# One expert's weights buffered ahead of the ring, copied in by VectorE, with the block work on ScalarE and GpSimd

## The reference

```python
e_idx = g_idx[:, None] * EXPERTS_PER_GROUP + loc        # top-1 group, top-2 experts in it, of 16
w = jnp.take_along_axis(scores, e_idx, axis=1); w = w / w.sum(-1, keepdims=True)
for e in range(N_EXPERTS):
    g_, u_ = jnp.split(t @ w_gu[e], 2, axis=-1)          # w_gu[e]: 1024 x 1024
    out = out + gates[:, e:e+1] * ((silu(g_) * u_) @ w_dn[e])   # w_dn[e]: 512 x 1024
```

## Time and profile before

| | |
|---|---|
| Median of 3 runs | 2003.49 us (1999.81 to 2008.18) |
| The profiled execution | 2015.61 us, its span 2013.8 us |
| Busy: PE, DVE, ACT, POOL | 1714.7, 641.6, 331.9, 129.3 us |
| Blocks of layer 0 | from about 809 to 1193 us of the span |
| Blocks of layer 1 | from about 1680 to 1981 us |

### The profile page before, as it was taken

The page is one execution under the profiler, slowest core; times in us unless marked ns, Lnnn a source line. Parts: engine busy times, 40 slices in busy tenths (PEclk is TensorE's granted clock), DMA queues, the critical chain, the costliest instruction groups (busy, mean ns, idle before and its releaser), DMA issues.

```text
span 2013.8 us, 29796 instructions
## 1 busy us (share of the span) xinstructions
PE 1714.7 (85%) x12508; PEld 1001.9 (50%) x12508; DVE 641.6 (32%) x1538; ACT 331.9 (16%) x730; POOL 129.3 (6%) x149
## 2 busy tenths in 40 slices
PE   5999999999999996789877755999989976777852
PEld 2454566554444585344433324767778863333311
DVE  3089336671110136101100005764641133000003
ACT  1001135521000102111110101014520020110100
POOL 0200000000000001111111110000000001111100
PEclk9999999999999997999989976999999987899976
DMA  9524545602123324674489984332015534889894
GB/s 308 139 84 140 195 157 184 192 23 87 54 72 94 104 76 184 247 299 159 158 312 350 365 281 133 108 104 74 1 52 160 171 133 163 342 326 361 340 365 152
DMA packets 188823, 365.06 MB, mean 181 GB/s; under 512 B 23285, under 2 KB 107773, under 8 KB 187923
## 3 DMA queue, kind: packets, MB, share of 16 engines
q1 hardware_dynamic: 176784, 331.48, 46.9%
q0 software_dynamic: 10704, 25.16, 3.6%
q10 hardware_dynamic: 1203, 6.51, 0.9%
HBM read 356.79 MB, written 14.42 MB: 184 GB/s over the span
## 4 chain that ended last, share of the span: by engine, by line
PE 67%; DMA 20%; DVE 7%; SPq 3%; ACT 2%; issue 1%; another core or an unknown queue 0%; DVEq 0%; POOLq 0%; ACTq 0%
PE psum L782 64%; DMA ring<-in_moe_w_gu 14%; DMA ring<-in_moe_w_dn 3%; SPq L669 2%; SPq L645 1%; PE psum L966 1%; PE psum L1176 1%; DMA arena<-ys 1%; DMA ring<-in_w_mod 1%; DVE arena L1802 1%; PE psum L1199 0%; PE psum L844 0%; ACT uT L1290 0%; DVE H L2058 0%; DMA ys<-qkT,y_row 0%
## 5 line engine op out<-in xcount | busy, mean ns | idle before, releaser
L782 PE MATMUL psum<-uT,ring 128*128 128x512 f32 (+1 forms) x1472 | 505.2, 503 | 3.3 <-ACT uT L1290 3.3
L782 PE MATMUL psum<-ring,mo_tok 128*32 128x256 f32 x4992 | 351.9, 408 | 110.3 <-DMA ring<-in_moe_w_gu 104.4
L782 PEld LDWEIGHTS psum<-uT,ring 128*128 128x128 f32 x1472 | 281.1, 192 | 222.8 <-issue 204.1
L782 PEld LDWEIGHTS psum<-ring,mo_tok 128*32 128x32 f32 x4992 | 145.7, 114 | 267.3 <-DMA ring<-in_moe_w_gu 167.7
L782 PE MATMUL psum<-ring,v_tok 128*32 128x256 f32 x2496 | 177.2, 419 | 33.3 <-DMA ring<-in_moe_w_dn 26.9
L2032 DVE TENSOR_TENSOR qkT<-psum,qkT 128x128 f32<-128x128 f32 x78 | 22.8, 292 | 404.8 <-ACT qkT L1493 280.1
L782 PEld LDWEIGHTS psum<-ring,v_tok 128*32 128x32 f32 x2496 | 81.3, 121 | 119.2 <-DMA ring<-in_moe_w_dn 46.9
L1672 DVE SCALAR_TENSOR_TENSOR convT<-upad,cwT,convT 128x512 f32<-128x512 f32 (+1 forms) x240 | 132.4, 614 | 2.1
L736 POOL DMA_INDIRECT ys<-qkT,y_row x78 | 77.4, 992 | 592.3 <-ACT qkT L1500 572.0
L782 PE MATMUL psum<-ring,uT 128*128 128x256 f32 (+1 forms) x576 | 113.7, 357 | 0.0
L1500 ACT ACTIVATE qkT<-psum,mqk 128x256 f32<-128x256 f32 x78 | 37.0, 474 | 457.6 <-PE psum L782 457.6
(11 more groups left out here) (284 smaller groups left out, 1428.2 us busy)
## 6 DMA issues: line engine op xcount, KB each, us to landing
ring<-in_moe_w_gu SPq DMA_DIRECT2D x256, 512.0 KB, 7.5
ring<-in_moe_w_dn SPq DMA_DIRECT2D x128, 512.0 KB, 6.7
ring<-in_w_in SPq DMA_DIRECT2D x104, 512.0 KB, 4.7
ring<-in_w_mod SPq DMA_DIRECT2D x96, 512.0 KB, 6.2
ring<-in_w_out SPq DMA_DIRECT2D x16, 512.0 KB, 4.5
ring<-in_w_a_out SPq DMA_DIRECT2D x8, 512.0 KB, 3.5
ring<-in_w_b_out SPq DMA_DIRECT2D x8, 512.0 KB, 4.5
ring<-in_w_c_out SPq DMA_DIRECT2D x16, 256.0 KB, 3.0
```

The costliest lines, as they stand in the source:

```text
L782: return nc.tensor.matmul(dst, lhsT, rhs, start=start, stop=stop)
```

## The change

- Twelve staging buffers of a part each are laid over `yab`, `uT` and `arena`. SyncE fills them for expert 1 as soon as the last reader of each is done (the last branch projection, the last transposes of the tokens, the stored token rows), and for expert e > 1 once part x of expert e-1 has been copied out. Expert 0 goes straight into the ring as before.
- VectorE copies each part from staging into the ring once it is staged (`w_staged[x]`) and the last block of the expert before has used that part (`w_used[x]`), and counts up `w_loaded[x]`. It reads `blocks_to` for that, once an expert, where SyncE did.
- ScalarE also copies the up half of the block from PSUM to SBUF (`gated_blk`), does `hidden_copy`, and both halves of each quad copy but the first, whose second half stays on VectorE.
- GpSimd does the product `hidden`, out of SBUF, one block ahead of the store in its queue.
- `r_cover`, a scratch row of the routing, moves from `yab` to `convT`.

```diff
+        gated_blk = qkT[:, 2, 2 * P:4 * P].rearrange("p (u c) -> p u c", u=2)
+        staging = [buf[:, 2 * x:2 * x + 2, :].rearrange("p a b -> p (a b)") for buf in (yab, uT, arena) for x in range(4)]
...
-        r_cover = yab[0:1, 0:2, :].rearrange("p a b -> p (a b)")[:, 0:MAX_BLOCKS * NE].rearrange("p (b e) -> p b e", e=NE)
+        r_cover = convT[0:1, 0:2, :].rearrange("p a b -> p (a b)")[:, 0:MAX_BLOCKS * NE].rearrange("p (b e) -> p b e", e=NE)
...
-                for e in range(NE):
-                    if e == 1:
-                        sp.wait_ge(counted, l + 1)
-                    if e:
-                        before_e = sp.value_load(blocks_to[0:1, e - 1:e], min_val=1, max_val=n_blocks[l])
+                for x in range(NX):
+                    n = index[("expert", l, x // 2)]
+                    if x % 2 == 0:
+                        sp.wait_ge(stream[n - NS][1], stream[n - NS][2])
+                    sp.dma_start(ring[:, n % NS, (x % 2) * D:(x % 2 + 1) * D], parts[x][0]).then_inc(w_loaded[x], 16)
+                nt = token_tiles(l)
+                for e in range(1, NE):
                     for x in range(NX):
-                        n = index[("expert", l, x // 2)]
-                        if e:
-                            sp.wait_ge(w_used[x], before_e + blk_base[l])
-                        elif x % 2 == 0:
-                            sp.wait_ge(stream[n - NS][1], stream[n - NS][2])
-                        sp.dma_start(ring[:, n % NS, (x % 2) * D:(x % 2 + 1) * D], parts[x][e])\
-                            .then_inc(w_loaded[x], 16)
+                        if e > 1:
+                            sp.wait_ge(w_loaded[x], 16 * (NE * l + e))
+                        elif x == 0:
+                            wait_ready(sp, "yb", l, KD - 1)
+                        elif x == 4:
+                            wait_ready(sp, "nat", l, nt - 1, 1)
+                        elif x == 8:
+                            for t in range(nt):
+                                sp.wait_ge(us_stored[t], 16 * (l + 1))
+                        sp.dma_start(staging[x], parts[x][e]).then_inc(w_staged[x], 16)
...
+                def hidden(b):
+                    u = b % 2
+                    pool.wait_ge(silu_ready, base + b + 1)
+                    if b >= 2:
+                        pool.wait_ge(hidT_ready, base + b - 1)
+                    nc.gpsimd.tensor_tensor(hid_blk[:, u, :], gated_blk[:, u, :], silu_blk[:, u, :], ALU.mult)\
+                        .then_inc(up_drained, 1)
+
+                hidden(0)
                 for b in range(nb):
+                    if b + 1 < nb:
+                        hidden(b + 1)
...
-                    f(silu_blk[:, b % 2, :], psum[G_BANK[b % 2]][:, 0:P], ACT.Silu).then_inc(silu_ready, 1)
+                    f(silu_blk[:, b % 2, :], psum[G_BANK[b % 2]][:, 0:P], ACT.Silu)
+                    f(gated_blk[:, b % 2, :], psum[G_BANK[b % 2]][:, P:2 * P], ACT.Copy).then_inc(silu_ready, 1)
...
+                        hidden_copy(b - 1)
                     if b % QUAD == 0 and b // QUAD + 1 < nquad:
-                        quad_copy(b // QUAD + 1)
+                        quad_copy(b // QUAD + 1, 0)
+                        quad_copy(b // QUAD + 1, 1)
...
+                dve.wait_ge(counted, l + 1)
+                for e in range(1, NE):
+                    before_e = dve.value_load(blocks_to[0:1, e - 1:e], min_val=1, max_val=n_blocks[l])
+                    for x in range(NX):
+                        dve.wait_ge(w_staged[x], 16 * ((NE - 1) * l + e))
+                        dve.wait_ge(w_used[x], before_e + blk_base[l])
+                        n = index[("expert", l, x // 2)]
+                        v.tensor_copy(ring[:, n % NS, (x % 2) * D:(x % 2 + 1) * D], staging[x]).then_inc(w_loaded[x], 16)
```

More of the change, by code:

```diff
@@ L449, in build @@
         w_loaded = [sem(f"expert_part_loaded{x}") for x in range(NX)]
+        w_staged = [sem(f"expert_part_staged{x}") for x in range(NX)]
         w_used = [sem(f"expert_part_used{x}") for x in range(NX)]
@@ L731, in dispatch_and_collect @@
                         pool.wait_ge(gathered[t], 16)
+                base = blk_base[l]
+                def hidden(b):
[6 more added lines that the diff above has]
+                hidden(0)
                 for b in range(nb):
+                    if b + 1 < nb:
+                        hidden(b + 1)
                     if b % QUAD == 0 and b // QUAD + 2 < nquad:
                         gather_quad(b // QUAD + 2)
[L735 removed]
+                    pool.wait_ge(down_drained, base + b + 1)
                     pool.indirect_dma_start(ys, bass.IndirectOffsetOnAxis(y_row[:, b:b + 1], 0), y_blk[:, b % 2, :], None,
@@ L1479, in _, with quad_copy, hidden_copy @@
                 base, qbase = blk_base[l], quad_base[l]
-                def quad_copy(p):
-                    act.wait_ge(quads_ready[0], qbase + p + 1)
+                def quad_copy(p, i):
+                    act.wait_ge(quads_ready[i], qbase + p + 1)
                     if p >= 2:
                         act.wait_ge(up_ready, base + QUAD * (p - 1))
-                    f(xT_blk[:, p % 2, 0:4, :], psum[X_BANK[0]][:, :].rearrange("p (k t) -> p k t", k=4), ACT.Copy)\
-                        .then_inc(quads_drained[0], 1)
+                    f(xT_blk[:, p % 2, 4 * i:4 * i + 4, :], psum[X_BANK[i]][:, :].rearrange("p (k t) -> p k t", k=4), ACT.Copy)\
+                        .then_inc(quads_drained[i], 1)
+                def hidden_copy(b):
+                    act.wait_ge(hidT_ready, base + b + 1)
+                    if b >= 2:
+                        act.wait_ge(down_ready, base + b - 1)
+                    f(hT_blk[:, b % 2, :], psum[H_BANK[b % 2]][:, 0:P], ACT.Copy).then_inc(hidT_drained, 1)
                 def silu(b):
@@ L1503, in _ @@
                 act.wait_ge(rows_used, 2 * l + 2)
-                quad_copy(0)
+                quad_copy(0, 0)
                 for b in range(nb + 1):
@@ L2014, in _ @@
                 gain_and_bias(2 * l + 1)
[L2017 to L2047, removed]
+                dve.wait_ge(quads_ready[1], quad_base[l] + 1)
+                v.tensor_copy(xT_blk[:, 0, 4:8, :], psum[X_BANK[1]][:, :].rearrange("p (k t) -> p k t", k=4))\
+                    .then_inc(quads_drained[1], 1)
+                dve.wait_ge(counted, l + 1)
[6 more added lines that the diff above has]
+                        v.tensor_copy(ring[:, n % NS, (x % 2) * D:(x % 2 + 1) * D], staging[x]).then_inc(w_loaded[x], 16)
                 for x in range(nt):
```

## The result

| | before | after |
|---|---|---|
| Median of 4 runs each | 2005.71 us (1999.81 to 2008.18) | 1884.40 us (1883.58 to 1886.55) |
| The profiled execution, its span | 2015.61 us, 2013.8 us | 1886.55 us, 1884.8 us |
| Blocks of layer 0, first gate/up matmul to last output copy | 808.94 to 1192.30, 383.4 us | 810.67 to 1118.25, 307.6 us |
| Blocks of layer 1, the same | 1680.28 to 1980.50, 300.2 us | 1603.49 to 1850.80, 247.3 us |

The ratio is 0.9401, its 95% interval 0.9376 to 0.9425. Forecast were 1901 us and a range of 1872 to 1946. The table's last rows say where the 129.0 us of the two spans lie: 75.8 in the blocks of layer 0, 52.9 in those of layer 1.

The account below looks back on a forecast made before the run. TensorE waits for expert weights while DMA also stands still. 2015.6 - 66 (layer 0) - 41 (layer 1) + 1 (start) + 2 (product) + 1 (tails) = 1912.6; less 12.1 to the median, 1900.5, said as 1901 us; range 1872 to 1946.

Parts of the forecast that it names:

- the two kinds of holes: DMA idles during experts with many blocks, and between two-block experts, where down parts are asked for late.
- The full stretches of 1.03: Sign in the changed profile: DMA share near 1.0 from about 995 to 1120 and from 1690 to 1934 us.
- Two of the signs: VectorE's ring copies 0.8 us at most; GpSimd's product under 0.6 us, over 1 us counting against the prediction.
- The stream: Loading one expert's weights at full DMA share: 17.3 us, seven streams ending layer 0, fourteen in layer 1.
- Rival 3: A faster weight stream, 16.6 us an expert: 17 us less, 1884 us; chance 0.16.
- The road to expert 7's last block: Layer 0: expert 4's first Silu at 878.2, then PE's pace, 6.07 us a block, to 995.7 instead of 1029.76.
- The step from the profiled execution to the median: End of the sum: the median of the runs lies 12.1 us under the profiled execution, so 1912.6 becomes 1900.5.
- The copies: VectorE's staging-to-ring copies, 180 a layer: 0.8 us each, twelve 9.7 us, covered by DMA, cost zero.
- The product: Gate product on GpSimd: 0.5 us, 0.1 us late a block, mattering in 19 PE-paced blocks: 2 us.
- Rival 2: GpSimd's product late: 0.99 plus 0.8 waiting for a copy, 1.4 us in 19 PE-bound blocks, 27 us: 1932; chance 0.12.
- rival 1: The weight stream does not fill: 18.8 us an expert, 24 streams cost 36 us more, 1937 us; chance 0.16.
- The start: Start of layer 0's blocks: early staging loads collide with the token gather of 797.98, costing 1 us.

Follow-up runs that it names:

- run 1: Changed kernel without staging: SyncE fills the ring as before, block work stays on GpSimd and ScalarE; 2006.54 us, ratio 0.9988.
- run 3: Changed kernel, each staged part of experts 1 to 15 loading only 512 of its 1024 columns, copies whole; 1818.39 us, ratio 0.9052.
- run 4: Changed kernel with each ring copy made as a reduction over an axis of one element, 1.21 us instead of 0.69; 1885.06 us, ratio 0.9387.
- run 5: Changed kernel with ring copies as slower reductions and half the columns of each staged part left out; 1844.89 us, ratio 0.9181.
- Run 7: Changed kernel with each part copied twice from staging to the same place in the ring; 1954.22 us, ratio 0.9715.
- run 6: Changed kernel with each ring copy made in two halves of 512 columns; 1886.67 us, ratio 0.9391.
- run 10: Changed kernel with eighteen staging buffers instead of twelve and ring copies as slower reductions; 1873.09 us, ratio 0.9308.

## Why the prediction was right

**The mechanism.** Runs 1 and 3 carry it: no staging, no gain; half the bytes, 66 us less. Of the two kinds of holes the change closes the one between experts of two blocks. Beside the experts with many blocks it loads one expert ahead, but DMA still stands idle then: from 900 to 980 us its share is 0.58 at a PE that is 0.97 busy. The full stretches of 1.03 were named beforehand and are there. So is the end of PE's waits for weights: from 876 to 992 us, in experts 4 to 7 of layer 0, 1.5 us of waits for a ring copy are left. Two of the signs are not as named: single copies take up to 1.00 us, and the longest product takes 1.01 us, just over the 1 us that was to count against the prediction; its mean is 0.65.

**The sum.** In the profiled executions the forecast was 1912.6 - 2015.6, 103 us less; measured were 129. The mechanism was right; the sizes were off, and two errors partly cancelled:

- *The stream*, put at 17.3 us, measured 16.5 (layer 1) and 16.7 (layer 0). This is the mis-sized term. Fourteen times 0.8 are 11 of the 12 us by which layer 1 gained more (52.9 for 41), seven times 0.6 are 4 of the 10 in layer 0 (75.8 for 66); 4 more come from the next point, and 1.7 from the later start, which the table counts to the head. I had chosen the rate of the long average, which held the holes in it, over the one full stretch of 13 us. A share of 1.01 with parts in the queue was the better sample: the holes were what the change removes. Rival 3, which took 16.6, had the right stream. That it gave 1884 to the microsecond is luck: between the profiled executions it had a gain of 120 us where 129 came, and the 9.9 us of the third point made up for that.
- *The road to expert 7's last block.* The first Silu of expert 4 was forecast at 878.2 and came at 875.77. The start of expert 7's last block was forecast at 995.7 and lies near 991.7 (a copy ahead of 992.48). The last copy was to end at 1120.6 and ended at 1112.3. Between expert 4's last Silu (924.22) and the one of expert 7's last block (997.24) lie twelve blocks, 73.0 us: 6.08 each, where 6.07 was taken from the earlier trace rows. That these agree is luck. The 6.07 held the late copy of 912.95 (a block of 6.4 us instead of 5.6, once in four), which the change takes away; the 6.08 hold late products in its place. With neither, in run 4, a block takes 5.90.
- *The step from the profiled execution to the median.* I took 12.1 us off for it. That supposes that the changed kernel's profiled execution lies as far above its median; it lies only 2.2 above, so the step took 9.9 us too much off. 26.0 us too little gain, less these 9.9, is the 16 between 1900.5 and 1884.4. Beside run 1 the blocks of before are 8.0 us longer in layer 0 and 3.2 in layer 1. How much of the 75.8 us is thus that execution's own is not shown, since run 1 also has the shorter PE-bound blocks.

**The copies.** 0.69 us in the median for 0.8, and up to 1.00. They are hidden: twelve are 8.3 us beside a stream of 16.5. At 1.23 a copy the prediction had 14.8 us a series; run 5 puts the pace of 1.21 us copies at 13.5. Run 7 shows what they cost once the cover is gone.

**The product.** 0.45 us for 0.5; the mean with the late ones is 0.65. Rival 2 had the right mechanism and the wrong worth. A product that meets a copy is late by up to 0.56 us, not by 0.8 more than 0.99, and in expert 4, the longest stretch at PE's pace, nearly all blocks are without copies, since the ring is full (a wait of 38.4 us of VectorE for PE). Experts 4 to 7 of layer 0 pay 2.8 us against run 4, where 2 was forecast and 27 by the rival. In the whole time runs 4, 6 and 10 find nothing, but in 4 and 10 the slower copies took the gain back, so what a copy as fast that doesn't hold the product would bring is not shown. The Trainium skill (SBUF — State Buffer, "SBUF: two separate sides") says that a copy in a two-port mode and a GpSimd operation lock one another out for a whole instruction. The runs agree: 1.01 us beside full copies, 0.77 beside halves, 0.47 at most beside reductions.

**The stream fills, against rival 1.** The period that it needed, 18.8 us, is not there. The Trainium skill (DMA: Bandwidth & Descriptors, "Where 436 GB/s comes from") has about 358 GB/s as HBM's limit for one core. The trace doesn't agree: 406 GB/s for 100 us and 407 for 216. The one core ran alone here; no run shows two.

**The start.** In layer 0 1 us was forecast and 1.7 came: the token rows' gather was waited for until 807.69 us and PE's first block began at 810.67. Among the kernels of this study that first matmul lies between 805.65 and 810.67 with no order to it, so this says little.

## What to carry over

A buffer filled ahead is worth the holes that it closes, so look for the moments when the transfer engine has nothing asked of it: size the gain with the rate of the fullest stretch, not with an average that holds the holes. A second copy on the way is free as long as a whole series of copies is shorter than a stream, but once it isn't, it costs more than the difference, since copies can't be made ahead. Half an expert more of staging paid another 15 us. Where one kernel's profile is the base of a sum, see first how far it stands from its own median. A pace that comes out as forecast can still be luck: here one delay had gone and another of the same size had come.

## What the hardware showed that was not expected

- GpSimd's 128x128 product takes 0.45 us, and waits for a running full-speed copy of VectorE (up to 1.01 us), but not for a reduction that moves the same data in 1.21 us (0.47 at most).
- The busy share misleads for short instructions back to back: VectorE was 0.90 busy in run 4 and still had 3 us of 16.5 to spare, since twelve copies of 1.21 us, 14.5 us by their durations, fit a period of 13.52.
- The issue of a block's store on GpSimd takes 1.14 us on average where it took 0.99, and up to 1.85 beside copies; with no staging it was at most 1.04.
